# Gated recurrence: the level products on 64x64 and 32x32 tiles of their masks, the merges over second halves

## What is computed

```
bc = cumsum(log_f)                       # decay, summed along the sequence
a[t, s] = sum_k q[t, k] * exp(b[t, k] - b[s, k]) * k[s, k]     for s <= t, else 0
o = (q * exp(b)) @ state + a @ v
state = exp(b_last) * state + (k * exp(b_last - b))^T @ v
```

## Time and profile before

| | us |
|---|---|
| runs (3), lowest, median, highest | 2730.15, 2736.87, 2737.28 |
| the profiled execution, its own time | 2736.06 |
| its span, from first to last instruction | 2734.0 |
| PE busy in it | 2654.2 |
| DVE busy | 1219.6 |
| ACT busy | 973.3 |
| POOL busy | 924.0 |
| mean granted TensorE clock, of full speed | 0.992 |

### The profile page before, as it was taken

The page is one execution under the profiler, slowest core; times in us unless marked ns, Lnnn a source line. Parts: engine busy times, 40 slices in busy tenths (PEclk is TensorE's granted clock), DMA queues, the critical chain, the costliest instruction groups (busy, mean ns, idle before and its releaser), DMA issues.

```text
span 2734.0 us, 34812 instructions
## 1 busy us (share of the span) xinstructions
PE 2654.2 (97%) x13470; PEld 2165.2 (79%) x13470; DVE 1219.6 (45%) x2033; ACT 973.3 (36%) x1397; POOL 924.0 (34%) x224
## 2 busy tenths in 40 slices
PE   8999999999999999999999899999998999999997
PEld 7898787888788877888877678888876767888886
DVE  6567533343521235101248853704533564370553
ACT  3353522222533334222243843212234774321222
POOL 2321343443232223444333134444432112444442
PEclk9999999999999999999999999999999999999999
DMA  7431334443222212222222022222221111222221
GB/s 311 185 139 63 122 147 153 168 171 114 88 70 70 70 62 74 88 100 95 86 97 78 16 85 93 92 103 97 92 85 46 48 47 70 92 93 107 92 92 62
DMA packets 44026, 270.84 MB, mean 99 GB/s; under 512 B 5071, under 2 KB 8679, under 8 KB 15752
## 3 DMA queue, kind: packets, MB, share of 16 engines
q1 hardware_dynamic: 39888, 265.71, 26.9%
q10 hardware_dynamic: 4024, 3.54, 0.6%
HBM read 267.09 MB, written 2.13 MB: 98 GB/s over the span
## 4 chain that ended last, share of the span: by engine, by line
PE 67%; issue 23%; POOL 5%; DVE 3%; ACT 2%; POOLq 0%; ACTq 0%; DVEq 0%
PE lin L726 20%; PE lin L728 19%; PE lin L727 19%; POOL wlo L675 5%; PE lin L1260 1%; PE bank L1244 1%; PE bank L1270 1%; PE lin L868 1%; PE bank L1429 0%; DVE small L2927 0%; DVE tmp L3075 0%; PE bank L885 0%; DVE pt L2941 0%; PE bank L1409 0%; PE lin L1409 0%
## 5 line engine op out<-in xcount | busy, mean ns | idle before, releaser
L675 POOL TENSOR_TENSOR wlo<-raw,whi 128x2048 fp32r<-128x2048 f32 (+3 forms) x212 | 918.6, 4333 | 1773.8 <-ACT whi L1751 1773.8
L726 PE MATMUL lin<-hhi,whi 128*128 128x512 f32 x1976 | 783.8, 397 | 11.0 <-DVE hlo L2559 2.5
L728 PE MATMUL lin<-hhi,wlo 128*128 128x512 f32 x1976 | 771.0, 390 | 0.0
L727 PE MATMUL lin<-hlo,whi 128*128 128x512 f32 x1976 | 770.7, 390 | 0.0
L1751 ACT ACTIVATE whi<-raw 128x2048 fp32r<-128x2048 f32 (+3 forms) x212 | 383.3, 1808 | 937.3 <-PE lin L728 873.0
L726 PEld LDWEIGHTS lin<-hhi,whi 128*128 128x128 f32 x1976 | 371.9, 188 | 103.2 <-issue 13.1
L726 PE MATMUL lin<-ghi,whi 128*128 128x512 f32 x1120 | 439.0, 392 | 4.3 <-POOL wlo L675 2.4
L728 PE MATMUL lin<-ghi,wlo 128*128 128x512 f32 x1120 | 436.5, 390 | 0.0
L727 PE MATMUL lin<-glo,whi 128*128 128x512 f32 x1120 | 436.4, 390 | 0.0
L728 PEld LDWEIGHTS lin<-hhi,wlo 128*128 128x128 f32 x1976 | 371.6, 188 | 79.0
L727 PEld LDWEIGHTS lin<-hlo,whi 128*128 128x128 f32 x1976 | 372.0, 188 | 74.8 <-issue 1.2
(11 more groups left out here) (472 smaller groups left out, 2824.9 us busy)
## 6 DMA issues: line engine op xcount, KB each, us to landing
raw<-in_w SPq DMA_DIRECT2D x171, 1024.0 KB, 4.8
adw_a<-in_ada SPq DMA_DIRECT2D x30, 1024.0 KB, 4.9
adw_b<-in_ada SPq DMA_DIRECT2D x18, 1024.0 KB, 6.1
raw<-in_w SPq DMA_DIRECT2D x20, 768.0 KB, 4.4
raw<-in_w SPq DMA_DIRECT2D x16, 640.0 KB, 3.9
raw<-in_w SPq DMA_DIRECT2D x5, 512.0 KB, 3.3
x<-in_x SPq DMA_DIRECT2D x1, 2048.0 KB, 16.9
out<-x SPq DMA_DIRECT2D x8, 256.0 KB, 2.0
```

The lines of the kernel that those rows point to most:

```text
L675: nc.gpsimd.tensor_tensor(wlo[:, slot, 0:size], raw[:, slot, 0:size], whi[:, slot, 0:size].bitcast(F32), ALU.subtract).then_inc(s.wlo_ok, 1)
L726: pe.matmul(dst, lh, rh, start=first, stop=False)
L727: pe.matmul(dst, lh, rl, start=False, stop=False)
L728: return pe.matmul(dst, ll, rh, start=False, stop=last)
```

## The change

In `level` the four full products become products of tiles. Level 1 keeps, for each chunk, keys 0 to 63 by queries 64 to 127 (one 64x64 tile); level 2 keys 0 to 31 by queries 32 to 63 and keys 64 to 95 by queries 96 to 127 (two 32x32 tiles); level 0 and levels 3 to 7 the four 32x32 tiles on the diagonal. A tile's keys are its output partitions, so a tile's weights are w columns of the array, all 128 rows. In `collect` the predicated copy of levels 1 to 7 reads and writes only the second half of each block of queries, 256 columns in place of 512, in runs of 64, 32, 16, 8, 4, 2 or 1. Level 0's copy stays.

```
-                        tk = slice(t * P, (t + 1) * P)
-                        mm = pe.matmul((B4, B5)[i % 2][:, tk], k_[:, tk], q_[:, tk], start=True, stop=True)
+                        for key, query in blocks:
+                            ks, qs = slice(t * P + key, t * P + key + w), slice(t * P + query, t * P + query + w)
+                            mm = pe.matmul((B4, B5)[i % 2][key:key + w, qs], k_[:, ks], q_[:, qs], start=True, stop=True)
```

```
+                    w = 64 if l == 1 else 32
+                    blocks = ((0, 64),) if l == 1 else ((0, 32), (64, 96)) if l == 2 else [(b, b) for b in range(0, P, 32)]
```

```
-                    mask = hmask[:, l * P:(l + 1) * P].unsqueeze(1).broadcast_to([P, TT, P])
-                    v.copy_predicated(by_tile(za[h % 2]), mask, by_tile((B4, B5)[i % 2][:, :])).then_inc(s.a_rd, 1)
+                    mask = hmask[:, l * P:(l + 1) * P]
+                    if l == 0:
+                        own = lambda ap: by_tile(ap)
+                        mask = mask.unsqueeze(1).broadcast_to([P, TT, P])
+                    else:
+                        own = lambda ap: ap.rearrange("p (t b two j) -> p t b two j", t=TT, two=2, j=LEVELS[l - 1])[:, :, :, 1, :]
+                        mask = halves(mask, LEVELS[l - 1])[:, :, 1, :].unsqueeze(1)\
+                            .broadcast_to([P, TT, P // (2 * LEVELS[l - 1]), LEVELS[l - 1]])
+                    v.copy_predicated(own(za[h % 2]), mask, own((B4, B5)[i % 2][:, :])).then_inc(s.a_rd, 1)
```

## The result

| | before | changed |
|---|---|---|
| median of 5 runs each, us | 2735.84 | 2723.11 |
| lowest to highest, us | 2730.15 to 2737.28 | 2720.65 to 2723.45 |
| profiled execution, us (span) | 2736.06 (2734.0) | 2723.45 (2721.4) |

The ratio is 0.995 with an interval of 0.9939 to 0.9962: 12.7 us faster, outside 0.3% as a whole.

A forecast was written before the change was run, and what follows sets the result against it. PE was taken to bound the heads, with DVE close behind. Terms of -6.5, -1.4, -0.6, -1.1 and +1.7 summed to -7.9 us, giving a forecast median of 2729 us, with 2724 to 2741 as the 8-in-10 range.

The forecast's parts named there:

- the upper end: Levels with 16 tiles: each record keeps 0.0275 us at 32 columns, slot 1.20 in place of 0.90, +7.2 us.
- the middle row: Levels with 16 tiles: instruction pace bounds 32 records at 0.009 to 0.010 us each, slot 0.63, -6.5 us; the estimate taken.
- the three theories: L1128's 32 records, first to last start: 0.2 us if strips fully overlap, 0.3 at instruction pace, 0.85 at 0.0275 each.
- the lower end: Levels with 16 tiles: four strips work at once, each held by its moving columns, 0.007 us a record, slot 0.54, -8.6.
- last copies: Head's end before L1207: the halved last copy takes about 0.46 us in place of 0.73, four times 0.27, -1.1 us.
- what is given back: Heads: +1.7 us lost again, 0.6 from DVE pacing levels 4 to 7 and 1.1 from loads not running ahead.
- an earlier end of the heads is passed on: Behind the heads: projections wait only 0.4 us in all for weights up to 420 us, so the heads' gain reaches the end.
- what becomes late next: Levels 4 to 7: DVE's step of 1.03 us against PE's 0.98, and loads that can't run ahead, together +1.7 us.
- I expect no price for the short runs: Strided copies: a copied half takes about 0.46 us at every run length, since multiplications with such runs stay near 417 ns.
- the rival with long copies: Collecting copies: a predicated copy with strided mask is no shorter, DVE's step stays 1.3, about -5 us, 2732; chance 0.08.
- The rival with a floor: Tiled levels: every record in tile form costs 0.0275 us whatever its columns, +4.9 us, 2741.8; chance 0.17.
- Full overlap: Tiled levels: strips work at once, held by their moving columns; -10.0 us after DVE takes back 1.7, 2727; chance 0.12.

The follow-up runs named there:

- packed_za: Changed kernel with the copies of levels 6 and 7 written contiguously into the first half of za (wrong result, for time alone); one execution of 2722.53 us.
- tiles_only: Changed kernel's tiled level products with the 128x512 collecting copies of the kernel before; 2722.41 us, ratio 0.9956 to before.
- strip_order: Changed kernel with the tile loop turned, blocks outside and chunks inside, so one strip's records follow each other; 2733.2 us, ratio 0.999 to before.

## Why the prediction was right and wrong

**Right: what bounds the heads, and that strips overlap.** PE sets the heads, and tiles on different strips run beside each other. That the old slot of 0.90 came from the records' weights rests on the earlier trace rows alone; no run tested it apart. The clock was 1.00 through the heads, a middle head is 13.3 where about 14 was named, and the upper end's price of 1.20 is right for the case that it was read from, 128 moving columns (1.21).

**Luck: the choice of the middle row.** The prediction took the pace at which the loads of `convolve` come, 0.009 to 0.010, and the trace has 0.008 on average, 0.26 from first to last start where 0.2, 0.3 and 0.85 were named for the three theories. The number is near, the cause is another: each strip takes a record about every 0.03, and four at once give 0.008. That is the lower end's picture, strips that work at once and each held by itself, with 0.03 in place of 0.0275 for the step of a strip; but the step is no longer set by the moving columns. For level 2 the prediction did count by strip, and its slot of 0.54 is near the 0.57 measured.

**The terms of the sum.**

| term | forecast | measured |
|---|---|---|
| levels with 16 tiles, 24 | slot 0.63, -6.5 | slot 0.58, -7.7 |
| level 2, four | slot 0.54, -1.4 | slot 0.57, -1.3 |
| level 1, four | slot 0.76, -0.6 | slot 0.81, -0.4 |
| last copies | -1.1 | wait at L1210 0.35 in place of 0.46: -0.4 |
| what is given back | +1.7 | none seen |
| heads | -7.9 | -10.2 |
| behind the heads | passed on one to one | -2.8: 1.1 of a wait, 1.7 of half clock; and -1.0 at 1402 us |

The measured terms of the heads sum to -9.8. What is missing are the late operands of levels 6 and 7 before, 0.22 in each of the first three heads, which are gone (-0.7); the prediction took every level at the 1.25 of level 3. Against it, the first head's level 0 lies ahead of the first copy and so outside what is called the heads here (+0.3). Outside the heads stand the start-up of the profiled execution, 1.4 later, and 1.0 from the half clock at 1402 us: -10.2 - 2.8 - 1.0 + 1.4 = -12.6.

**Wrong, the first step: "an earlier end of the heads is passed on".** It was read from waits up to 420 us and stopped there. The wait of 2.37 us at 463 us, and the half clock behind it, stood in the same view one stretch further. The step as such, an earlier end is passed on, holds; what fails is that the places behind the heads would stay as they were. With 608 more TensorE records the load of instructions that fell among the weights before falls behind them. I had named no cost or gain for that, nor for the stretches at half clock. They are 2.8 and 1.0 of the 4.7 us between the forecast and the profiled execution; the heads are 2.3, and the late start takes 1.4 off.

**Wrong, the second step: "what becomes late next", +1.7.** DVE does step at 1.00 against PE's 0.93, as worked out. But PE does not wait for it at a level: its steps over levels 5 to 7 are all 0.93 to 0.94, because the two banks and the operands made ahead leave room for 0.07 a step over so few levels. Nor is it paid later. The 0.35 at L1210 is the price of the two long copies, since in `packed_za`, with the same DVE step of 1.00 and short copies, it is not there. And the waits of 0.3 a head that I put on loads not running ahead were a guess from one row; none came.

**Wrong, the third: the copies.** "I expect no price for the short runs" was argued from the multiplications. It holds down to runs of 4 and fails for 2 and 1, and those are the last two copies of a head. So the last copy stays at 0.73, and the term of -1.1 came to -0.4. Nor was the last copy the only one on the path: before, the long copies of levels 4 and 5 made the operands of levels 6 and 7 late. Of the rival with long copies the condition was half met, for the last two levels only. `tiles_only` is that rival whole, and its heads are still 8.2 us shorter than before, where the prediction had about 5.

**The rivals.** The rival with a floor falls with 0.008 per record, far below the 0.018 from which it decides. A floor there is, but on each strip: 0.03 for 16 and for 32 columns. Where the strips do not take turns, `strip_order`, it turns 10 us of gain into none in the heads. The clock did not fall in the heads, with PE busy 54.18 of 56.00 us there at clock 1.00:

```profile
180.00:236.00 56.00, 54.18 (x1015) 43.76 (x1014) 44.90 (x113) 28.86 (x60) 0.00 (x0) 1.00 0.01 3
```

Full overlap, with a slot of 0.54 and -10.0, is nearest to what the heads did, and its mechanism is the one that the runs show, strips at work at once. Two of its sizes are off and partly cancel: the slot is 0.58, and the give-back of 1.7 is missing.

## What to carry to other kernels

Small tiles of a product pay when consecutive records go to different strips: the order of the loop was worth as much here as the whole change. Count the records of the strip that has most of them, here about 0.03 us each with 16 or 32 moving columns and 0.10 with 128, and add 0.3 to 0.4 us for going into tiles and out again (slot less first to last start). When an edit changes how many instructions run, read the long waits and the stretches at half clock of the whole kernel before you pass a gain on, not only those of the next stretch; and for a strided copy look at the shortest run of its output, above all where it is the last one before a wait.

## What the runs showed of the chip

- A strip of 32 columns took an fp32 record about every 0.03 us, alone, beside one other strip or beside three (on four strips in turn one started every 0.008 on average), and as often with 16 moving columns as with 32; with 128 it was 0.10. A half of the array with 64 columns took one every 0.058, alone or beside the other half.
- A predicated copy of 128x256 took 0.43 to 0.45 us with output runs of 4 and more elements and 0.73 with runs of 2 or 1, as much as one of 128x512. Runs in the mask and in the bank that it reads cost nothing, and a multiplication with the same runs stayed at 0.42.
- One load of 16 KB of instructions among 768 KB weight transfers goes with a landing 1.1 us later (8.3 against 7.2). The four traces with it, before among them, waited 2.1 us or more, and none of the ten without it more than 1.4 (six different numbers of TensorE records in all); the rest of the path from the landing to the wait was not taken apart.
